# Four-block transformer kernel: residual sums released bank by bank, and the second norm turned per token tile with the router's product between

## Chip, core and metric

The kernel runs on one core of a Trainium2 chip. The metric is the device time of one execution in microseconds (us). The kernel before takes 2551.68 us, the median of three runs from 2546.58 to 2554.73.

## The reference, cut to what matters

The input is 256 tokens of width 1024, all in 32-bit floats. A first block has two layers, each a mixer (gated delta rule, then dilated window attention) and a squared-ReLU MLP. A second block has two layers, each with three gated branches, an output product, and a mixture of 16 experts that choose their tokens. The residual stream `x` goes through a root-mean-square norm ahead of every part:

```
first block:  for i in 0, 1:
    x = x + mixer_i(rmsnorm(x, norm_mix[i]))
    x = x + square(relu(rmsnorm(x, norm_mlp[i]) @ w1)) @ w2
x = rmsnorm(x, norm_final)
second block: for l in 0, 1:
    h  = rmsnorm_2(x, norm1_g[l]) * (1 + sc1) + sh1
    x  = x + g1 * (merged(h) @ w_out[l])
    h2 = rmsnorm_2(x, norm2_g[l]) * (1 + sc2) + sh2
    aff = softmax(h2 @ w_router[l])          # 16 experts
    x  = x + g2 * experts(h2, top_k(aff))    # each expert takes its 32 best tokens
return rmsnorm_2(x, final_g)
```

A norm needs the sum of squares over a token's whole row of 1024 values, so it can't be finished before the last residual sum of that token.

## The kernel before, in words

**Tiles.** The 256 tokens stand as two tiles of 128, token on partition: `X[:, t, :]` is the residual of tile `t`, `XN` its normed copy, `HT` the normed copy turned to features on partitions (eight chunks `dc` of 128 features, 256 tokens wide). PSUM has eight banks of 512 columns. A product that ends in a residual fills banks 0 to 3: bank `b` holds tile `b // 2`, columns half `b % 2`. Its last weight unit is walked bank by bank (L819 to L827, L869 to L891, L1011 to L1028), so that bank 0 is complete first and bank 3 last.

**Weights.** They stream through a ring of six slots of 2 MB, loaded by SyncE's queue (L395 to L401). A slot is loaded anew when its user has raised `w_free`; each expert of the second block takes six units of 2 MB.

**Order of the work.** Each engine has its own instruction stream, written out by hand, and waits on semaphores with counts. VectorE (DVE), ScalarE (ACT), GpSimd (POOL) and TensorE (PE) share a norm as follows. ACT handles tile 0: when `x_half` says that the tile's residual is complete, it squares and sums it (L2016), forms the mean (L2018, `var0`), POOL takes it to the power -1/2 (L2415), and ACT scales the tile (L2033 or L2023, `xn0`). DVE handles tile 1 in the same way: L1332 squares and sums with one instruction over 1024 columns, L1335 forms the mean (`var1`), POOL takes the power, DVE scales (L1342 or L1363, `xn1`). PE turns eight chunks of each tile (`norm`, L565 to L574).

**Residual sums of the first block** (`residual`, L1366 to L1376, four times): DVE waits for `half_mm`, which PE raises when bank 1 is complete, and adds banks 0 and 1 to tile 0. Ahead of bank 2 it waits until the whole weight unit is used (`complete`, that is bank 3), and only then adds banks 2 and 3. After the first and the third residual the norm goes straight to an MLP (`norm_split`, L576 and L1361): tile 0 is turned and multiplied first, tile 1 only behind two products of tile 0. After the second and the fourth, the next step (`norm` for the window attention, the final norm of the first block) wants both tiles.

**Residual sums of the second block** (`gated_residual`, L1782 to L1797): each bank is multiplied by a gate row into `TMP` and then added, two instructions of 512 columns per bank, with a `drain` (`settle`) after each. It runs after the output product (L1926) and after the experts (L2000).

**The second norm** (L1929 to L1932 on DVE, L2374 on ACT, L1244 to L1250 on PE) stands between the output product and the router. DVE first forms the scale and shift columns `SCL` and `BIA`. PE's `norm` turns both tiles into banks 4 to 7, with both tiles of a chunk side by side. ACT applies scale and shift to chunks 0 to 3 and DVE to chunks 4 to 7, 256 columns each (L2037, L1349). PE waits for all eight and then multiplies the router weights: 16 products (tile by chunk) with 16 columns each (L1248), recorded as 32. ACT meanwhile rounds `XN` to a second copy (L2375) and DVE subtracts it (L1935). DVE's L1937 takes the row maximum of the router's result, and from there softmax, top-k, gather and the expert loop (L1273, first product L1284) follow.

## Time and profile before

| | |
|---|---|
| median of three runs | 2551.68 us |
| the profiled execution, its own time | 2548.41 us |
| span of its trace | 2546.4 us |
| PE busy | 2051.8 us, 81% |
| DVE busy | 864.3 us, 34% |
| ACT busy | 594.8 us, 23% |
| POOL busy | 32.0 us, 1% |
| read from memory | 639.21 MB, 251 GB/s over the span |

The span is the time from the first to the last instruction; the 2.0 us to the execution's own time lie around it. Busy shares are averages over stages with different limits. PE's granted clock in the profile is 1.0 at 2.4 GHz and 0.5 at 1.2 GHz.

### The profile page before, as it was taken

Reading aid. Unit: us, or ns where it says so; the run is one execution under the profiler, and the core shown is the slowest. Engines: PE = TensorE matmul, PEld = TensorE weight load, DVE = VectorE, ACT = ScalarE, POOL = GpSimd, SP = SyncE. Lnnn points to the kernel's source line nnn. Section 1 sums busy time; section 2 is a strip of 40 time slices with the busy share of each in tenths; the row PEclk is TensorE's granted clock in tenths of the full one; section 3 lists DMA queues with packets and bytes.
Section 4 is the critical chain, followed back from the end, with each engine's and each line's share of the span. In section 5 each row is a group of like instructions: output and inputs, shape, how many; then the busy total and the mean of one; then the engine's idle time right before and its main releaser. Section 6 shows DMA issues by size and latency. Waiting matters only on the chain.

```text
span 2546.4 us, 34316 instructions
## 1 busy us (share of the span) xinstructions
PE 2051.8 (81%) x14184; PEld 1362.8 (54%) x14184; DVE 864.3 (34%) x1599; ACT 594.8 (23%) x1001; POOL 32.0 (1%) x50
## 2 busy tenths in 40 slices
PE   7877889998998997999876666665999976666765
PEld 6756657877756885788542222222778652222221
DVE  4645564665554664244220000002144230010002
ACT  3222234441123442064210010001054120000000
POOL 0010000000000000000000000000000000000000
PEclk9989899998998998999888887887999988888787
DMA  8201034766963665432459999999332439999996
GB/s 309 102 1 35 2 109 155 265 242 208 329 240 137 251 250 176 149 133 100 165 223 427 426 427 425 426 427 387 134 132 93 201 153 426 427 426 427 426 426 283
DMA packets 150299, 641.76 MB, mean 252 GB/s; under 512 B 9310, under 2 KB 30840, under 8 KB 117046
## 3 DMA queue, kind: packets, MB, share of 16 engines
q1 hardware_dynamic: 143898, 637.13, 63.0%
q10 hardware_dynamic: 6300, 3.20, 0.5%
q8 instruction: 74, 1.21, 0.2%
q14 instruction: 27, 0.22, 0.0%
HBM read 639.21 MB, written 1.10 MB: 251 GB/s over the span
## 4 chain that ended last, share of the span: by engine, by line
PE 55%; DMA 31%; DVE 6%; ACT 3%; issue 2%; DVEq 1%; POOL 1%; SPq 0%; ACTq 0%; POOLq 0%
DMA ring<-in_w_down 31%; PE psum L1189 5%; PE psum L844 5%; PE psum L846 5%; PE psum L845 5%; PE psum L1304 4%; PE psum L1100 3%; PE psum L1089 3%; PE psum L942 3%; PE psum L616 2%; PE psum L1179 2%; PE psum L823 2%; PE psum L647 1%; PE psum L959 1%; PE psum L737 1%
## 5 line engine op out<-in xcount | busy, mean ns | idle before, releaser
L1284 PE MATMUL psum<-ring,arena 128*32 128x256 f32 x4096 | 298.0, 442 | 185.1 <-DMA ring<-in_w_up 146.1
L1284 PEld LDWEIGHTS psum<-ring,arena 128*32 128x32 f32 x4096 | 143.5, 123 | 341.5 <-issue 155.6
L1304 PE MATMUL psum<-ring,arena 128*32 128x512 f32 x1024 | 166.9, 784 | 94.1 <-DMA ring<-in_w_down 84.8
L844 PE MATMUL psum<-arena_r 128*128 128x512 f32 x512 | 207.8, 406 | 13.9 <-DVE arena_r L1650 7.1
L846 PE MATMUL psum<-ring_r,arena_r 128*128 128x512 f32 x512 | 205.0, 400 | 0.0
L1991 DVE TENSOR_TENSOR arena<-psum,arena 128x256 f32<-128x256 f32 x32 | 13.6, 425 | 559.0 <-PE psum L1284 559.0
L1384 DVE TENSOR_TENSOR ring_r<-ring,arena_r 128x2048 fp32r<-128x2048 f32 x64 | 143.8, 2288 | 87.0 <-ACT arena_r L2049 87.0
L2392 ACT ACT_TABLE_LOAD x32 | 41.1, 1283 | 514.3 <-PE psum L1284 514.3
L1998 DVE COPY arena<-psum 128x512 f32<-128x512 f32 x64 | 44.3, 692 | 273.0 <-PE psum L1304 271.8
L2049 ACT CAST arena_r<-ring 128x2048 fp32r<-128x2048 f32 x64 | 119.6, 1904 | 71.8 <-PE psum L846 71.8
L1304 PEld LDWEIGHTS psum<-ring,arena 128*32 128x32 f32 x1024 | 32.8, 126 | 191.4 <-DMA ring<-in_w_down 101.5
L1400 DVE SCALAR_TENSOR_TENSOR arena<-ring,c_act,arena 128x512 f32<-128x512 f32 x168 | 126.3, 752 | 12.5
L1313 PE MATMUL psum<-arena 128*128 128x512 f32 x256 | 127.0, 640 | 0.3
L844 PEld LDWEIGHTS psum<-arena_r 128*128 128x128 f32 x512 | 98.6, 193 | 37.5 <-issue 7.8
L1189 PE MATMUL psum<-x_normed_r,arena_r 128*128 128x256 f32 x384 | 116.5, 303 | 0.2
L846 PEld LDWEIGHTS psum<-ring_r,arena_r 128*128 128x128 f32 x512 | 98.0, 191 | 23.5
L1189 PE MATMUL psum<-x_normed_r,ring_r 128*128 128x256 f32 x384 | 108.5, 282 | 0.0
L1189 PE MATMUL psum<-h_featmajor_r,arena_r 128*128 128x256 f32 x384 | 107.2, 279 | 0.0
L845 PE MATMUL psum<-arena_r 128*128 128x512 f32 x256 | 103.1, 403 | 0.0
L845 PE MATMUL psum<-arena_r,h_featmajor_r 128*128 128x512 f32 x256 | 101.8, 397 | 0.0
L1313 PEld LDWEIGHTS psum<-arena 128*128 128x128 f32 x256 | 49.8, 207 | 92.9 <-issue 50.7
L616 PE MATMUL psum<-h_featmajor,ring 128*128 128x256 f32 x384 | 88.4, 385 | 1.8 <-DVE h_featmajor L1347 1.8
(379 smaller groups left out, 3026.1 us busy)
## 6 DMA issues: line engine op xcount, KB each, us to landing
ring<-in_w_gate SPq DMA_DIRECT2D x64, 2048.0 KB, 26.6
ring<-in_w_up SPq DMA_DIRECT2D x64, 2048.0 KB, 26.1
ring<-in_w_down SPq DMA_DIRECT2D x64, 2048.0 KB, 26.3
ring<-in_mlp_w SPq DMA_DIRECT2D x32, 2048.0 KB, 8.7
ring<-in_w_mod SPq DMA_DIRECT2D x24, 2048.0 KB, 11.2
ring<-in_w_in SPq DMA_DIRECT2D x20, 2048.0 KB, 8.1
ring<-in_gdn_w_in SPq DMA_DIRECT2D x8, 2048.0 KB, 17.9
ring<-in_dswa_w_in SPq DMA_DIRECT2D x9, 1536.0 KB, 14.4
```

The source lines that it names most:

```text
L616: ins = mm(bank(ch % 4, T), W(n, 512)[:, k, (ch % 4) * P:(ch % 4 + 1) * P], HT[:, k, :], start=k == 0, stop=k == KC - 1)
L844: mm(o, xh, wh, start=start, stop=False, skip_group_check=True)
L845: mm(o, xl, wh, start=False, stop=False, skip_group_check=True)
L846: return mm(o, xh, wl, start=False, stop=stop, skip_group_check=True)
L942: ins = mm(bank(n % 4, T), W(u, SCOLS)[:, k, (n % 3) * P:(n % 3 + 1) * P], HT[:, k, :], start=k == 0, stop=k == KC - 1)
L1189: ins = mm(o[:, 0], w[:, k, :], x[:, k, :], start=k == 0 and x is XH_R and w is wh, stop=k == KC - 1 and w is wl, skip_group_check=True)
L1284: ins = mm(PS[32 * j:32 * j + 32, 4 + m, 0:T], XGE[:, 4 * u + kk, :], W(v + 2 * m + u, D)[:, kk, j * T:(j + 1) * T], start=u == 0 and kk = ...
L1304: ins = mm(PS[32 * j:32 * j + 32, (7, 4)[half], :], HTE[:, k % 2, 32 * (k // 2):32 * (k // 2) + 32], W(v + 4 + u, D)[:, j, half * 512:(hal ...
L1313: ins = mm(bank(2 * t + u), S4[:, t * P:(t + 1) * P], YS[:, u, :], start=False, stop=False, skip_group_check=True)
L1384: v.tensor_tensor(ring_r[slot][:, at], ring[slot][:, at], WH[h % 4].bitcast(F32), ALU.subtract).then_inc(sem("w_lo"), 1)
L1400: ins = v.scalar_tensor_tensor(acc, w, CACT[:, k:k + 1], acc, ALU.mult, ALU.add)
L2049: a.copy(WH[h % 4], ring[mlp_unit(l, i) % RING][:, hf * HALF:(hf + 1) * HALF]).then_inc(sem("hi"), 1)
```

## The change

`half_mm` is raised twice per residual, for bank 1 and for bank 2, and DVE waits for each. Bank 2 is now added when it is complete; only bank 3 waits for the whole unit. For tile 1 the square and sum over 1024 columns is split into two of 512 columns (`square_part`), each run behind the sum of its bank; a small addition (`ssq_parts`) joins them in `mean_square`. This is used by the four residuals of the first block and by the output product's residual of the second block; the residual after the experts, the first norm of each layer of the second block, the very first and the very last norm keep the whole square (`parts=False`). In the second block `SCL` and `BIA` of the second norm are formed ahead of the residual. The second norm is turned per token tile (`norm_split` with `pm=True`): tile 0 into banks 4 and 5, tile 1 into banks 6 and 7. ACT scales all eight chunks of tile 0 and chunks 0 to 3 of tile 1, DVE chunks 4 to 7 of tile 1, 128 columns each. PE turns tile 0, then tile 1, then multiplies the router with tile 0, waits for tile 1's chunks, and multiplies the router with tile 1.

```diff
@@ PE: rows_product, mlp down, out_steps alike
-                    if last and (kk, b) == (cnt - 1, 1):
+                    if last and kk == cnt - 1 and b in (1, 2):
                         ins.then_inc(sem("half_mm"), 1)
@@ PE: second norm and router
+                def router(t):
+                    for k in range(KC):
+                        ins = mm(PS[:, 4, t * NE:(t + 1) * NE], HT[:, k, t * P:(t + 1) * P], WR[:, k, :], start=k == 0, stop=k == KC - 1)
+                    return ins
...
-                norm(L * 2 + 5, True)
-                normed(L * 2 + 7)
-                for t in range(TT):
-                    for k in range(KC):
-                        ins = mm(PS[:, 4, t * NE:(t + 1) * NE], HT[:, k, t * P:(t + 1) * P], WR[:, k, :], start=k == 0, stop=k == KC - 1)
-                ins.then_inc(sem("router_mm"), 1)
+                for t in range(TT):
+                    norm_split(L * 2 + 5, t, True)
+                    if t == 1:
+                        pe.wait_ge(sem("ht0_ready"), L + 1)
+                        router(0)
+                pe.wait_ge(sem("ht_ready"), L * 16 + 48 + 16)
+                router(1).then_inc(sem("router_mm"), 1)
@@ DVE: norm
+            def square_part(h):
+                xs = X[:, 1, h * 512:(h + 1) * 512]
+                v.tensor_tensor_reduce(out=XN[:, 1, h * 512:(h + 1) * 512], in0=xs, in1=xs, scale=1.0, scalar=0.0,
+                                       op0=ALU.mult, op1=ALU.add, accum_out=ssq_parts[:, h:h + 1])
+            def mean_square(r, meanwhile=None, parts=True):
+                if parts:
+                    settle()
+                    v.tensor_tensor(ssq[:, 1:2], ssq_parts[:, 0:1], ssq_parts[:, 1:2], ALU.add)
+                else:
+                    v.tensor_tensor_reduce(out=XN[:, 1, :], in0=X[:, 1, :], in1=X[:, 1, :], scale=1.0, scalar=0.0,
+                                           op0=ALU.mult, op1=ALU.add, accum_out=ssq[:, 1:2])
                 settle()
                 v.tensor_scalar(var[:, 1:2], ssq[:, 1:2], 1.0 / D, EPS, ALU.mult, ALU.add).then_inc(sem("var1"), 1)
@@ DVE: residual
-                dve.wait_ge(sem("half_mm"), n)
+                dve.wait_ge(sem("half_mm"), 2 * n - 1)
                 for b in range(4):
                     t, h = b // 2, b % 2
                     if b == 2:
-                        ins.then_inc(sem("x_half"), 1)
+                        dve.wait_ge(sem("half_mm"), 2 * n)
+                    elif b == 3:
                         complete()
                     xs = X[:, t, h * 512:(h + 1) * 512]
                     ins = v.tensor_tensor(xs, bank(b), xs, ALU.add)
-                ins.then_inc(sem("x_ready"), 1)
+                    if b == 1:
+                        ins.then_inc(sem("x_half"), 1)
+                    elif b == 3:
+                        ins.then_inc(sem("x_ready"), 1)
+                    if b >= 2:
+                        settle()
+                        square_part(h)
@@ DVE: gated_residual
                     ins = v.tensor_tensor(xs, xs, TMP, ALU.add)
                     if b == 1:
                         ins.then_inc(sem("x_half"), 1)
+                    elif b == 3:
+                        ins.then_inc(sem("x_ready"), 1)
+                    settle()
+                    if b >= 2 and parts:
+                        square_part(h)
+                    if b == 1:
+                        tile1_first()
+                    elif b == 2:
                         tile1_ready()
-                    elif b < 3:
-                        settle()
-                ins.then_inc(sem("x_ready"), 1)
                 settle()
@@ DVE: second norm
-                dve.wait_ge(sem("half_mm"), L + 5)
-                gated_residual(L * 2 + 1, lambda: (settle(), spent(dve, u2 + V_OUT + 1, tu)))
                 v.scalar_tensor_tensor(SCL, mc(4), 1.0, PMC[:, bass.ds(L * 8 + PM_AT["norm2_g_2"], 8)], ALU.add, ALU.mult)
                 v.tensor_copy(BIA, mc(3))
-                settle()
-                norm(L * 2 + 6, L * 2 + 7, lambda dc: SCL[:, dc:dc + 1], lambda dc: BIA[:, dc:dc + 1])
+                dve.wait_ge(sem("half_mm"), L * 2 + 9)
+                gated_residual(L * 2 + 1, lambda: dve.wait_ge(sem("half_mm"), L * 2 + 10), lambda: spent(dve, u2 + V_OUT + 1, tu), True)
+                mean_square(L * 2 + 6)
+                v.tensor_scalar(XN[:, 1, :], X[:, 1, :], rstd[:, 1:2], None, ALU.mult).then_inc(sem("xn1"), 1)
+                dve.wait_ge(sem("ht_psum"), L * 3 + 9)
+                for dc in range(4, KC):
+                    v.tensor_scalar(HT[:, dc, P:T], PS[:, 7, (dc % 4) * P:(dc % 4 + 1) * P], SCL[:, dc:dc + 1], BIA[:, dc:dc + 1],
+                                    ALU.mult, ALU.add).then_inc(sem("ht_ready"), 1)
@@ ACT: second norm
-                norm(L * 2 + 6, L * 2 + 7, L * 2 + 6, lambda dc: SCL[:, dc:dc + 1], lambda dc: BIA[:, dc:dc + 1])
+                mean_square(L * 2 + 6, L * 2 + 6)
+                act.wait_ge(sem("rstd_ready"), (L * 2 + 6) * 2 + 1)
+                a.activation(XN[:, 0, :], X[:, 0, :], ACT.Copy, scale=rstd[:, 0:1]).then_inc(sem("xn0"), 1)
+                for t in range(TT):
+                    act.wait_ge(sem("ht_psum"), L * 3 + 8 + t)
+                    for dc in range(KC - 4 * t):
+                        ins = a.activation(HT[:, dc, t * P:(t + 1) * P], PS[:, 4 + 2 * t + dc // 4, (dc % 4) * P:(dc % 4 + 1) * P],
+                                           ACT.Identity, scale=SCL[:, dc:dc + 1], bias=BIA[:, dc:dc + 1])
+                        if t == 1:
+                            ins.then_inc(sem("ht_ready"), 1)
+                    if t == 0:
+                        ins.then_inc(sem("ht0_ready"), 1)
                 a.copy(XNH_R, XN[:]).then_inc(sem("xn_hi"), 1)
```

## Rows read from the trace of the kernel before

**Rows 1.** The page, its chain that ended last: shares of the span.
```profile
PE 55%; DMA 31%; DVE 6%; ACT 3%; issue 2%; DVEq 1%; POOL 1%; SPq 0%; ACTq 0%; POOLq 0%
```

**Rows 2.** The same chain in order of time: start us, us, what.
```profile
1225.57 20.70 PE psum L823 x48
...
1338.24 26.59 DMA ring<-in_w_down
```

**Rows 3.** Timeline, layer 0's second norm: start us, us, engine, line, operation [idle before <-releaser].
```profile
1253.15 0.69 DVE L1788 TENSOR_TENSOR arena<-psum,arena 128x512 f32<-128x512 f32 x1 [3.79 <-PE psum L823]
...
1253.92 0.69 DVE L1790 TENSOR_TENSOR x_resid<-x_resid,arena 128x512 f32<-128x512 f32 x1
...
1256.81 1.23 DVE L1332 CUSTOM_DVE_ANT_0 x_normed<-x_resid 128x1024 f32<-128x1024 f32 x1
...
1258.48 0.15 DVE L1335 TENSOR_SCALAR var<-ssq 128x1 f32<-128x1 f32 x1 [0.43 <-issue]
...
1260.10 1.97 PE L573 MATMUL psum<-base,x_normed 128*128 128x128 f32 x8 [6.10 <-DVE x_normed L1342]
1262.11 1.93 ACT L2037 ACTIVATE h_featmajor<-psum,norm_shift,norm_scale 128x256 f32<-128x256 f32 x4 [9.39 <-PE psum L573]
...
1264.10 7.01 PE L1248 MATMUL psum<-arena,h_featmajor 128*128 128x16 f32 x32 [2.02 <-ACT h_featmajor L2037]
...
1265.86 2.29 DVE L1935 TENSOR_TENSOR x_normed_r<-x_normed,arena_r 128x2048 fp32r<-128x2048 f32 x1 [1.85 <-ACT arena_r L2375]
1271.14 0.19 DVE L1937 TENSOR_REDUCE arena<-psum 128x2 f32<-128x32 f32 x1 [2.99 <-PE psum L1248]
```

**Rows 4.** Timeline, DVE: a square of 512 columns elsewhere, and two small instructions with a drain between.
```profile
672.21 0.69 DVE L1695 CUSTOM_DVE_ANT_0 arena<-psum,arena 128x512 f32<-128x512 f32 x1 [1.39 <-PE psum L980]
...
1272.46 0.17 DVE L1939 RECIPROCAL arena<-arena 128x2 f32<-128x2 f32 x1 [1.12 <-ACT act_junk L2380]
1272.70 0.37 DVE L1942 TENSOR_SCALAR arena<-arena 128x16 f32<-128x16 f32 x2
```

**Rows 5.** Timeline, the second residual (ahead of the window attention).
```profile
585.65 1.29 DVE L1375 TENSOR_TENSOR x_resid<-psum,x_resid 128x512 f32<-128x512 f32 x2 [4.29 <-PE psum L846]
...
588.38 0.15 DVE L1335 TENSOR_SCALAR var<-ssq 128x1 f32<-128x1 f32 x1
...
590.00 1.97 PE L573 MATMUL psum<-base,x_normed 128*128 128x128 f32 x8 [3.52 <-DVE x_normed L1342]
```

**Rows 6.** Timeline, the third residual (ahead of the second MLP).
```profile
770.12 2.48 DVE L1375 TENSOR_TENSOR x_resid<-psum,x_resid 128x512 f32<-128x512 f32 x4
...
772.73 1.23 DVE L1332 CUSTOM_DVE_ANT_0 x_normed<-x_resid 128x1024 f32<-128x1024 f32 x1
773.03 1.84 POOL L2415 TENSOR_TENSOR rstd<-var,neg_half 128x1 f32<-128x1 f32 x2 [183.88 <-ACT var L2018]
...
774.39 1.15 ACT L2023 ACTIVATE x_normed<-x_resid,rstd 128x1024 f32<-128x1024 f32 x1 [1.44 <-POOL rstd L2415]
```

**Rows 7.** Timeline, the first residual (ahead of the first MLP).
```profile
378.16 0.56 POOL L2415 TENSOR_TENSOR rstd<-var,neg_half 128x1 f32<-128x1 f32 x1 [21.77 <-ACT var L2018]
...
381.08 2.18 ACT L2027 ACTIVATE arena_r<-psum,param_cols 128x128 fp32r<-128x128 f32 x8 [1.18 <-PE psum L583]
...
382.25 2.16 DVE L1358 SCALAR_TENSOR_TENSOR h_featmajor_r<-psum,param_cols,arena_r 128x128 fp32r<-128x128 f32 x8 [0.57 <-ACT arena_r L2027]
```

**Rows 8.** Stretches of layer 0's second norm: busy us by engine, granted clock, DMA share, GB/s.
```profile
1256.00:1260.00 4.00, 0.00 (x0) 0.00 (x0) 2.55 (x7) 0.00 (x0) 0.55 (x1) 0.73 1.00 422
```

**Rows 9.** Timeline: first expert product of layer 0, row maximum and first expert product of layer 1.
```profile
1299.95 7.11 PE L1284 MATMUL psum<-ring,arena 128*32 128x256 f32 x128 [1.88 <-DVE arena L1984]
...
2048.93 0.19 DVE L1937 TENSOR_REDUCE arena<-psum 128x2 f32<-128x32 f32 x1 [2.99 <-PE psum L1248]
...
2074.93 5.39 PE L1284 MATMUL psum<-ring,arena 128*32 128x256 f32 x96 [1.87 <-DVE arena L1984]
```

**Rows 10.** Timeline, DVE at the start of layer 1, behind the loop's branch.
```profile
1768.07 1.23 DVE L1332 CUSTOM_DVE_ANT_0 x_normed<-x_resid 128x1024 f32<-128x1024 f32 x1 [5.97 <-issue]
```

More of the change, by code:

```diff
@@ L885, in down @@
                         ins = three(bank(b), MTH_R[:, k, ts], MT_R[:, k, ts], wh[:, c], wl[:, c], first and k == 0, last and k == 3)
-                        if last and (b, k) == (1, 3):
+                        if last and k == 3 and b in (1, 2):
                             ins.then_inc(sem("half_mm"), 1)
@@ L1024, in out_steps @@
                              start=i == 0 and kk == 0, stop=i == 2 and kk == 2, skip_group_check=True)
-                    if i == 2 and (b, kk) == (1, 2):
+                    if i == 2 and kk == 2 and b in (1, 2):
                         ins.then_inc(sem("half_mm"), 1)
@@ L1081, in _ @@
                 norm(L * 2 + 4, True)
[L1082 removed]
+                pe.wait_ge(sem("ht_ready"), L * 16 + 48 + 8)
                 def tok(n, w, b):
@@ L1338, in mean_square, with norm @@
                 dve.wait_ge(sem("rstd_ready"), r * 2 + 2)
-            def norm(r, j, scale, shift=None, meanwhile=None):
-                mean_square(r, meanwhile)
+            def norm(r, j, scale, shift=None, meanwhile=None, parts=True):
+                mean_square(r, meanwhile, parts)
                 v.tensor_scalar(XN[:, 1, :], X[:, 1, :], rstd[:, 1:2], None, ALU.mult).then_inc(sem("xn1"), 1)
@@ L1414, in _ @@
             dve.wait_ge(sem("cols_ready"), 4)
-            norm(0, 0, lambda dc: colof("norm_mix", dc))
+            norm(0, 0, lambda dc: colof("norm_mix", dc), parts=False)
             dve.wait_ge(sem("filled"), 1)
@@ L1817, in columns @@
                     v.memset(CZ[:, :, 257:258], 0.0).then_inc(sem("gcol"), 1)
-                norm(L * 2 + 5, L * 2 + 6, lambda dc: SCL[:, dc:dc + 1], lambda dc: BIA[:, dc:dc + 1], meanwhile=columns)
+                norm(L * 2 + 5, L * 3 + 6, lambda dc: SCL[:, dc:dc + 1], lambda dc: BIA[:, dc:dc + 1], meanwhile=columns, parts=False)
                 for t in range(TT):
@@ L1999, in _ @@
                 dve.wait_ge(sem("expert_done"), L * NE + NE + 1)
-                gated_residual(L * 2 + 2, settle)
-            mean_square(9)
+                gated_residual(L * 2 + 2, settle, settle, False)
+            mean_square(9, parts=False)
             dve.wait_ge(sem("fgr_in"), 32)
@@ L2285, in _ @@
                 u2 = U_SEC
-                norm(L * 2 + 5, L * 2 + 6, L * 2 + 5, lambda dc: SCL[:, dc:dc + 1], lambda dc: BIA[:, dc:dc + 1])
+                norm(L * 2 + 5, L * 3 + 6, L * 2 + 5, lambda dc: SCL[:, dc:dc + 1], lambda dc: BIA[:, dc:dc + 1])
                 for dc in range(0, KC, 4):
```

12 lines of the change are left out of this document (4 added, 8 removed).

## The prediction

> **What bounds the kernel now.** I read the page first. The chain that ended last is PE for 55% of the span, DMA for 31%, DVE for 6% [rows 1]: two regimes. In the order of time the DMA part is the expert loop, where each expert waits some 27 us for its last weights [rows 2]; ahead of it everything follows PE, with short pieces of DVE, ACT and POOL wherever a norm stands between two products. So a norm costs what PE idles there, and in the expert loop only the start matters: the ring holds six units, which is one expert, so no further load can begin before the first expert product frees a slot. A start that is earlier by so much shifts the whole DMA-paced loop by as much.
>
> Then the timeline of each norm. In layer 0's second norm the last residual work begins at 1253.15, as PE ends its product, and the row maximum behind the router starts at 1271.14 [rows 3]: 18.0 us, of which PE's turn of tile 1 and the router take 1.97 and 7.01, and the rest is mostly waiting. Layer 1 repeats it: its row maximum stands at 2048.93, at the same distance [rows 9].
>
> **The second norm, part by part (twice).** Before, from 1253.15 to the mean at 1258.48 it is 5.33 us: two multiplications and two additions of 512 columns, at 0.77 each from start to start (1253.15 to 1253.92), `SCL` and `BIA`, and a whole square of 1.23 [rows 3]. After the change, bank 2's pair and its half square run while PE fills bank 3. That cover is real: the last 48 products of L823 take 20.70 us, 0.43 each [rows 2], a bank is 8 of them, 3.4 us, and the three instructions need 3 x 0.77 = 2.3. Were it gone, those 2.3 us would come back. `SCL` and `BIA` go in front of the residual, where DVE waits for PE. What stays behind PE's end: multiplication 0.77, addition 0.77, half square 0.77, small addition 0.24. The half square is priced by the 0.69 of the same instruction over 512 columns plus the drain of 0.08, the small addition by two small instructions with a drain between, 1272.46 to 1272.70 [rows 4]. Together 2.55, so 2.78 is gained. Of the old 5.33, some 0.35 are an idle of 0.43 ahead of the mean that no releaser explains [rows 3] and that may stay: bounds 2.4 and 2.8, taken 2.6.
>
> Then PE. Before, it turns tile 1 (1.97), idles 2.02 until eight chunks are scaled, and runs the router for 7.01 [rows 3]. After, router(0) follows the turn at once, 3.5 us, half of 7.01. Under it ACT and DVE scale four chunks each of 128 columns, 4 x 0.27 = 1.1 by eight of them in 2.18 [rows 7]; so router(1) follows without a gap and the 2.0 us are gone. Tile 0's eight chunks, 2.2 us on ACT, fit between tile 0's turn and tile 1's, where ACT waited 9.39 [rows 3]. The wait for `xn1` now stands at the head of PE's queue with router(0) behind it; that delays the router by nothing against before. ACT's rounding and DVE's subtraction, queued ahead of the row maximum, end later than their old distance: 1.1, 1.8 for the copy (1262.11 + 1.93 to 1265.86) and 2.29 [rows 3], 5.2 behind the turn; the router needs 7.0. They stay covered by 1.8, and are late next. Sum per layer 2.6 + 2.0 = 4.6, for two layers **9.2**. No DMA is issued earlier or later against its own slot, and SP's and POOL's orders stay.
>
> **The four residuals of the first block.** In the second, DVE's two last additions start at 585.65 and the mean at 588.38: 2.73 us, and PE idles 3.52 for it [rows 5]. After: one addition 0.77, half square 0.77, small addition 0.24, together 1.78. Two drains that now stand twice in a row cost about 0.05 each, estimated from the 0.08 between instructions; gain **0.9**. The fourth residual repeats the pattern, ahead of the final norm: another **0.9**. At the first, nothing: DVE waits 0.57 for ACT's tile 0 before it can go on [rows 7], so tile 0's path sets PE's start and tile 1's earlier mean is idle; its price is 0, or up to 0.8 lost if a half square got into POOL's way.
>
> The third is different: DVE comes late, all four additions run in a row from 770.12, and the whole square from 772.73 to 773.96 lies over POOL's power for tile 0, which begins at 773.03. The two powers take 1.84 together where one alone takes 0.56 [rows 6, 7]; ACT goes on at 774.39, 1.36 behind POOL's start. After the change, additions of banks 0 to 2 (0.60 apart) end at 772.0, the half square at 772.8, the fourth addition at 773.5, the second half square starts at 773.6. POOL's 773.03 to 773.59 falls under the addition, which reads PSUM. ACT then starts 0.6 behind 773.03: gain **0.76**. If the second half square catches POOL after all, ACT starts 0.43 behind that square's end, as it does now (773.96 to 774.39), at about 774.75: a loss of 0.36. I take the gain, since the addition is longer than POOL's 0.56; the margin is only 0.04.
>
> Here a rule speaks against the change. The Trainium skill, "GPSIMD Engine Reference", section Key points, says that GpSimd shares its SBUF interfaces with VectorE and contends with VectorE instructions that have two SBUF inputs; the half squares are such. By that rule the trace agrees at the third residual (1.84 against twice 0.56), and if it caught POOL there again the sum would be 1.1 smaller. In the second norm, too, bank 2's addition and half square could hold tile 0's power by up to 2 x 0.77 = 1.5; tile 0 has 9.39 us to spare [rows 3], so it costs nothing there.
>
> **Small losses.** The experts' residual gets a few more drains, 0.1 us at each of two places: -0.2.
>
> **Sum.** 9.2 + 0.9 + 0.9 + 0.76 - 0.2 = 11.6 us. The profiled execution took 2548.41 (span 2546.4), 3.3 below the median of 2551.68; against its own time 2536.8, against the median **2540.1 us**. About 0.3%, 7.7 us, is what a measurement of this kernel can tell from no change, since three runs lie 8 us apart.
>
> **Rivals.**
> *PE's clock stays up (0.15).* In 1256 to 1260 the mean granted clock is 0.73 with PE idle [rows 8]: since the turn of tile 0: it fell from 2.4 to 1.2 GHz at about 1257.8. With a gain of 2.6, tile 1's turn begins at about 1257.5. If the clock holds, turn and router halve (1.0 + 3.5 for 1.97 + 7.01), but the subtraction then bounds: its end moves by 1.0 only, so 1.8 + 1.0 = 2.8 a layer, 5.6 in all: 2534.5. Against it: after an idle of 3.52 the turn took 1.97, the slow value, in the second residual, too [rows 5].
>
> *Part of it is given back (0.20).* From row maximum to first expert product layer 0 takes 28.8 us and layer 1 26.0, with the same instructions [rows 3, 9]. If the changed order puts both layers on the slower side, 2.8 are lost; with POOL caught (1.1) and the idle ahead of the mean kept (0.35 twice) the gain is 7.0: 2544.7. That the change doesn't do what it says, PE leaving the 2.0 us in place in both layers, would give 2544.1 and lies here too.
>
> *Slower, by instruction supply (0.05).* At the start of layer 1, behind the loop's branch, DVE waits 5.97 us for nothing that the profile shows [rows 10], and in the second norm 0.43 in the same way, where the DMA share is 1.00 [rows 3, 8]. DVE's code changes length. If a wait like that of rows 10 came to stand in the second norm in both layers, 11.9 us would be lost, which just outweighs the gain; from the second such wait on the kernel is slower, and with a third at the start of layer 1 it is 17.9 - 11.6 = 6.3 slower: 2558.0. Against it: nothing in the straight code waits longer than 0.43 in the rows. The Trainium skill, "Runtime: NRT & Kernel Launch", section Instruction fetch mechanics, says that crossing a block of instructions in straight code is mostly hidden and that a taken branch to a page not at hand stalls. By that rule the sum stays 2540.1, as both kernels have the same branch; rows 10 agree.
>
> **How the numbers follow.** The forecast has 0.60, the rivals 0.15, 0.20 and 0.05. The scatter of the runs, about 4 to either side, goes on each case. From the clock's 2534.5, less a little, to the partial case's 2544.7 plus 4: range 2532 to 2549. Faster by more than 0.3% is below 2544.0: most of the forecast (0.51 of 0.60), the clock's 0.15 and a quarter of the partial case, 0.70. Within 0.3%: the rest of these, 0.26. Slower by more: 0.04, the last rival with scatter.
>
> **What would show it.** Right: in the second norm the mean 2.6 us behind PE's product instead of 5.3, no idle between the turn of tile 1 and the router, row maximum some 13.4 us behind PE's product end instead of 18.0; PE's idle in the second residual 2.6 instead of 3.52; POOL's first power in the third 0.56 long. Wrong: a wait of several us ahead of DVE's mean, the subtraction ending behind the router, or an expert loop whose first load doesn't start earlier by the same 4.6 us.

## The result, and the profile after

The changed kernel takes **2533.44 us**, the median of six runs from 2523.41 to 2540.30; six runs of the kernel before beside them have 2551.42 (2546.58 to 2554.73). The ratio is 0.9927, with a 95% interval from 0.9905 to 0.9949: some 18 us less. The forecast was 2540.1 in a range of 2532 to 2549. Sign and places were right; the gain is half as large again as the 11.6 us of the sum, and the median lies 1.4 us above the lower end of the range. The profiled execution took 2529.94 us (span 2527.8), 18.5 below the 2548.41 of the execution that was profiled before.

First the second norm of layer 0 in the timeline of the kernel after, which answers to [rows 3], with two lines of layer 1 behind it. PE's product ends as DVE's last multiplication begins, at 1246.02. The columns, here and in the other timelines: start, duration, engine, line, operation, out<-in, count, idle before it and what ended that.

```profile
1246.02 0.69 DVE L1812 TENSOR_TENSOR arena<-psum,arena 128x512 f32<-128x512 f32 x1 [1.16 <-PE psum L823]
1246.79 0.69 DVE L1814 TENSOR_TENSOR x_resid<-x_resid,arena 128x512 f32<-128x512 f32 x1
1247.61 0.69 DVE L1340 CUSTOM_DVE_ANT_0 x_normed<-x_resid 128x512 f32<-128x512 f32 x1
...
1248.43 0.16 DVE L1347 TENSOR_TENSOR ssq<-ssq_parts 128x1 f32<-128x1 f32 x1
1248.67 0.15 DVE L1352 TENSOR_SCALAR var<-ssq 128x1 f32<-128x1 f32 x1
...
1250.30 1.97 PE L583 MATMUL psum<-base,x_normed 128*128 128x128 f32 x8 [3.43 <-DVE x_normed L1960]
1252.06 6.84 PE L1240 MATMUL psum<-arena,h_featmajor 128*128 128x16 f32 x32
...
1252.30 1.37 DVE L1963 TENSOR_SCALAR h_featmajor<-psum,norm_scale,norm_shift 128x128 f32<-128x128 f32 x4 [2.06 <-PE psum L583]
1253.69 1.91 ACT L2418 CAST arena_r<-x_normed 128x2048 fp32r<-128x2048 f32 x1
...
1255.62 2.29 DVE L1967 TENSOR_TENSOR x_normed_r<-x_normed,arena_r 128x2048 fp32r<-128x2048 f32 x1 [1.96 <-ACT arena_r L2418]
1258.94 0.19 DVE L1969 TENSOR_REDUCE arena<-psum 128x2 f32<-128x32 f32 x1 [1.02 <-PE psum L1240]
...
2020.41 1.52 PE L583 MATMUL psum<-base,x_normed 128*128 128x128 f32 x8 [3.43 <-DVE x_normed L1960]
...
2028.61 0.19 DVE L1969 TENSOR_REDUCE arena<-psum 128x2 f32<-128x32 f32 x1 [1.02 <-PE psum L1240]
```

The mean stands 2.65 us behind PE's product end (1246.02 to 1248.67) instead of 5.33. The router begins inside the modelled end of tile 1's turn, with no idle of PE between them. The row maximum comes 12.92 behind the product's end instead of 17.99, and its wait of 1.02 ends with PE: DVE's subtraction, queued ahead of it, is done 1.0 earlier and stays covered as the prediction said, though by 1.0 and not by 1.8. In layer 1 the same distance is 2016.14 to 2028.61, 12.47. There tile 1's turn took 1.52, with a granted clock of 1.00 at its start and 0.50 at its end; in layer 0 it took 1.97 at 0.50 throughout. So the two norms gave 5.07 + 5.52 = 10.6 us.

Then the residuals of the first block, again from the timeline after: the second, which answers to [rows 5], and the third, which answers to [rows 6].

```profile
580.56 0.69 DVE L1393 TENSOR_TENSOR x_resid<-psum,x_resid 128x512 f32<-128x512 f32 x1 [1.29 <-PE psum L846]
581.38 0.69 DVE L1340 CUSTOM_DVE_ANT_0 x_normed<-x_resid 128x512 f32<-128x512 f32 x1
...
582.44 0.15 DVE L1352 TENSOR_SCALAR var<-ssq 128x1 f32<-128x1 f32 x1
...
584.07 1.97 PE L573 MATMUL psum<-base,x_normed 128*128 128x128 f32 x8 [2.67 <-DVE x_normed L1359]
...
765.28 1.88 DVE L1393 TENSOR_TENSOR x_resid<-psum,x_resid 128x512 f32<-128x512 f32 x3
...
767.90 0.69 DVE L1393 TENSOR_TENSOR x_resid<-psum,x_resid 128x512 f32<-128x512 f32 x1
768.20 0.55 POOL L2458 TENSOR_TENSOR rstd<-var,neg_half 128x1 f32<-128x1 f32 x1 [184.97 <-ACT var L2050]
768.72 0.69 DVE L1340 CUSTOM_DVE_ANT_0 x_normed<-x_resid 128x512 f32<-128x512 f32 x1
768.78 1.15 ACT L2055 ACTIVATE x_normed<-x_resid,rstd 128x1024 f32<-128x1024 f32 x1 [0.66 <-POOL rstd L2458]
```

In the second, from the first addition behind PE's product end to the mean it is 1.88 instead of 2.73 (one addition is left there instead of two), and PE idles 2.67 instead of 3.52: 0.85. The fourth repeats it (978.81 to 980.69). In the third POOL's power for tile 0 lies under an addition and takes 0.55 alone; ACT starts 3.50 behind the first addition instead of 4.27: 0.77.

These places sum to 10.6 + 0.85 + 0.85 + 0.77, less 0.1 at each end of the expert loops (the four pairs take 4.72 instead of 4.62 from first to last addition): **12.9 us**. The other 5.6 of the profiled 18.5 lie where the change touches nothing, 4.8 of them ahead of DVE's first addition of the first residual, called the front below: this stretch in the kernel before, in the kernel after, and in the kernel after a second time (its experiment follows), each from its own view of stretches (start:end, length, then busy time of PE, PEld, DVE, ACT and POOL, the granted clock, the DMA share, GB/s).

```profile
9.85:375.25 365.40, 299.80 (x3393) 234.66 (x3394) 202.01 (x491) 99.96 (x275) 17.85 (x21) 0.91 0.26 91
```

```profile
9.77:370.38 360.61, 292.80 (x3393) 228.84 (x3394) 201.90 (x492) 100.03 (x275) 17.85 (x21) 0.92 0.26 93
```

```profile
9.78:376.45 366.67, 298.24 (x3393) 233.41 (x3394) 201.97 (x492) 99.83 (x275) 17.85 (x21) 0.91 0.26 91
```

PE's 3393 products are the same; their busy time and the granted clock are not. The front of the profiled execution had the half clock for less of its time, some 54 us against 68 in the first row and 65 in the third (worked out from the granted clock in slices of 3 us). What that is worth was the main question for the runs.

### The profile page after: what moved, and what is told of

The parts are those of the page before. It is cut to its first block, busy times and chain, and to the rows that moved or that the text cites. A ratio compares the mean times of both kernels' runs of the same rounds, so it can differ in the third digit from the quotient of the medians.

```text
span 2527.8 us, 34370 instructions
## 1 busy us (share of the span) xinstructions
PE 2038.3 (81%) x14184; PEld 1355.8 (54%) x14184; DVE 864.9 (34%) x1617; ACT 599.8 (24%) x1017; POOL 31.3 (1%) x50
## 3 DMA queue, kind: packets, MB, share of 16 engines
q8 instruction: 74, 1.21, 0.2%
## 4 chain that ended last, share of the span: by engine, by line
PE 55%; DMA 32%; DVE 6%; ACT 3%; issue 2%; DVEq 1%; POOL 0%; SPq 0%; ACTq 0%; POOLq 0%
DMA ring<-in_w_down 31%; PE psum L1189 5%; PE psum L844 5%; PE psum L845 5%; PE psum L846 5%; PE psum L1311 4%; PE psum L1100 3%; PE psum L1089 3%; PE psum L942 3%; PE psum L616 2%; PE psum L1179 2%; PE psum L823 2%; PE psum L959 1%; PE psum L647 1%; PE psum L1275 1%
## 5 line engine op out<-in xcount | busy, mean ns | idle before, releaser
L616 PE MATMUL psum<-h_featmajor,ring 128*128 128x256 f32 x384 | 86.6, 379 | 1.8 <-DVE h_featmajor L1364 1.8
## 6 DMA issues: line engine op xcount, KB each, us to landing
ring<-in_w_up SPq DMA_DIRECT2D x64, 2048.0 KB, 26.2
```

The costliest lines, as they stand in the source:

```text
L616: ins = mm(bank(ch % 4, T), W(n, 512)[:, k, (ch % 4) * P:(ch % 4 + 1) * P], HT[:, k, :], start=k == 0, stop=k == KC - 1)
```

## Experiments

The edits are condensed, `...` marks lines that are left out, and each stands against the changed kernel where nothing else is said.

**The changed kernel and the kernel before, each once more.** No edit. Expected of the first:

> The changed kernel once more, for a second trace of it. In the first trace the stretch ahead of the first residual, which the change does not touch, was 4.9 us shorter than before (DVE's first addition at 370.38 instead of 375.25). Theory A (the front scatters from execution to execution with PE's clock, and the change is worth the 12 to 13 us that its own places show): the addition lies anywhere between 369 and 377, and the time about 12 to 18 us under the kernel before. Theory B (the front follows the code: the changed kernel always has it shorter): the addition lies within 0.5 of 370.4 again, and the time 18 us under the kernel before. The places of the change read the same in both: mean 2.65 behind PE's product end and row maximum 12.9 in layer 0, idle of PE ahead of tile 1's turn 2.67 in the second residual.

and of the second:

> The kernel before, for a second trace of it. Theory A: DVE's first addition of the first residual lies anywhere between 369 and 377, and what differs from the first trace of this kernel by more than 0.3 us in any stretch has a different granted clock there. Theory B: it lies within 0.5 of 375.25 again. Ratio 1.000, from 0.997 to 1.003.

The changed kernel took 2534.70 (ratio 0.9942, 0.9921 to 0.9962), the kernel before 2552.42 (1.0005, 0.9993 to 1.0017). The first addition came at 376.45 in the changed kernel, at 376.96 in the kernel before: Theory A. Within the front the same line shows what changed; the two rows are of the two executions of the changed kernel.

```profile
165.76 2.10 PE L737 MATMUL psum<-arena 128*128 128x128 f32 x16 [2.13 <-DVE arena L1619]
```

```profile
166.52 3.41 PE L737 MATMUL psum<-arena 128*128 128x128 f32 x16 [2.13 <-DVE arena L1619]
```

Sixteen equal products take 2.10 at a granted clock of 1.00 or 3.41 at 0.56. The two fronts of the kernel before, 365.4 and 367.1, have the same mean clock of 0.91 to the digits shown, so the difference in the mean that Theory A expected of them did not appear; single lines do differ (the 48 products of L616 take 12.37 and 10.63). Over the fourteen traces of this study the front takes 360.6 to 368.7 us; the kernel before lies inside with 365.4 and 367.1. So the 4.8 us that the front seemed to give were luck of one profiled execution. The places of the change repeat in the mean (2.65) and in PE's idle in the second residual (2.68), but layer 0's row maximum comes 12.18 behind the product's end and not 12.9: tile 1's turn took 1.22 there, at a granted clock near 1, behind the same idle of 3.43.

**The second norm alone.** The first block's residuals are as before:

```diff
 def residual(n, complete):
     dve.wait_ge(sem("half_mm"), 2 * n - 1)
     for b in range(4):
-        if b == 2: dve.wait_ge(sem("half_mm"), 2 * n)
-        elif b == 3: complete()
+        if b == 2: ins.then_inc(sem("x_half"), 1); complete()
...
-        if b >= 2: settle(); square_part(h)
```

> Only the second norm of the two layers is changed (banks released one by one, halved squares, tile 1 turned with the router's first half behind it); the four residuals of the first block are as before. Theory A: the gain is 5.07 + 5.52 = 10.6 us as the two row maxima showed, so 2541 against 2551.5, and the front has the length of one of the other traces by chance. Theory B: the shorter front needs the changed first block, so the front's addition stays at 375.2, and 10.6 us are all. A third theory, that the layers' code alone sets the phase of the front, would give 370.4 there and some 2536.

2539.93 against 2550.70 (ratio 0.9948, 0.9928 to 0.9967): 10.8 by the medians. From bank 0's addition to the row maximum it is 18.54 and 18.46 instead of 24.00, 11.0 us in all, as Theory A has it. The front was a short one (first addition at 371.46), so it needs no changed first block; but the stretch from there to layer 0's second norm was 877.5, 5.6 longer than in the kernel before, and took it back.

**The first block's residuals alone**, measured twice. The second norm goes back to the old order (the edit in part):

```diff
-    for t in range(TT):
-        norm_split(L * 2 + 5, t, True)
-        if t == 1: pe.wait_ge(sem("ht0_ready"), L + 1); router(0)
-    pe.wait_ge(sem("ht_ready"), L * 16 + 48 + 16)
-    router(1).then_inc(sem("router_mm"), 1)
+    norm(L * 2 + 5, True)
+    normed(L * 2 + 7)
+    router(0); router(1).then_inc(sem("router_mm"), 1)
```

> Only the four residuals of the first block are changed (banks released one by one, halved squares); the second norm stays whole, behind the old order of waits, but for its residual's wait, which now counts the bank releases. Theory A: the gain is 0.85 + 0.85 in the second and fourth residual, 0.25 net behind the third (0.77 at its first turn, of which the clock took back 0.5) and 0.24 at the first, 2.2 in all, so 2549; within 0.3 per cent of the kernel before. Theory B: the front is shorter by 4.9 too, 7 us in all, 2544.5. PE's idle in the second residual is 2.67 by both, row maximum 18.0 behind the product's end by both.

> The kernel with only the first block's four residuals changed, once more: its median lay 5.7 us under the kernel before, while its own places show 0.85 + 0.85 + 0.8 there and 0.35 at each second norm (the 0.43 us of idle ahead of the mean was gone), 3.2 in all. Theory A (the rest is scatter of PE's clock in stretches that the code does not touch): the ratio lies between 0.9975 and 0.9995 this time, and the sum over the places is 3.2 again. Theory C (the shorter idles of the first block make the clock come back earlier in what follows, so that the gain is larger than at the places): the ratio is 0.997 to 0.998 again and the time at the half clock between the first residual and layer 0 is smaller than the 60.3 us of the kernel before by 6 or more.

2545.01 against 2550.70 (0.9972, 0.9958 to 0.9985), then 2544.23 against 2551.30 (0.9962, 0.9947 to 0.9976): 5.7 and 7.1 us. The places gave what was expected, 0.85, 0.85 and 0.8, and each row maximum came 23.65 behind bank 0's addition instead of 24.00, as the idle of 0.43 ahead of the mean was gone: 3.2. So the first expectation, 2549, was too slow, and the second, a ratio of at least 0.9975, failed as well. Theory C is not borne out. Time at the half clock between the first residual and layer 0's second norm, worked out from the granted clock in slices of 3 us, is 68 and 58 us here, against 65 in both traces of the kernel before: more in one execution and less in the other. What differs in both is a later stretch, with the same instructions: from layer 0's row maximum to its first expert product it is 28.8 in both traces of the kernel before, and 25.9 and 24.7 here.

**The same stretch reached at another moment.** The kernel before, with products of zeros that move layer 0 and touch nothing behind (the edit against the kernel before, in part):

```diff
+    pe.wait_ge(sem("x_half"), L * 2 + 5)
+    for _ in range(4):
+        mm(bank(0), zero1.to_broadcast([P, P]), zero1.to_broadcast([P, 512]), start=True, stop=False, ...)
     norm(L * 2 + 4, True)
```

> The kernel before, with four products of zeros (512 columns, into bank 0 while it is free) in PE's idle ahead of each layer's first norm, and nothing of the change. The zeros are work added. They move layer 0 earlier by some 1.5 us (the turns of its first norm at the full clock) and leave the code of the second norm and behind it as it was. In both traces of the kernel before, 28.8 us lie between layer 0's row maximum and its first expert product; in the kernels with only the first block changed, 25.9 and 24.7, with the same instructions. Theory A (when the clock comes back in that stretch depends on the moment at which it is reached): the stretch is not 28.8 here, but anything from 24.5 to 29.0; the time 1.5 to 6 us under the kernel before. Rival (it is the kernel before that has 28.8 there, and the change that takes it away): 28.8 within 0.2, and 1.5 us under the kernel before at most. From bank 0's addition to the row maximum 24.00 by both.

2547.28 against 2552.32 (0.9977, 0.9967 to 0.9987). The timeline has the row maximum and the first expert product of both layers:

```profile
1272.03 0.19 DVE L1945 TENSOR_REDUCE arena<-psum 128x2 f32<-128x32 f32 x1 [2.99 <-PE psum L1256]
...
1298.09 7.12 PE L1292 MATMUL psum<-ring,arena 128*32 128x256 f32 x128 [1.88 <-DVE arena L1992]
...
2047.16 0.19 DVE L1945 TENSOR_REDUCE arena<-psum 128x2 f32<-128x32 f32 x1 [2.99 <-PE psum L1256]
...
2076.19 7.12 PE L1292 MATMUL psum<-ring,arena 128*32 128x256 f32 x128 [1.88 <-DVE arena L1992]
```

Layer 0's stretch is 26.06 now, and layer 1's, which was 26.0 before, is 29.03: neither the layer nor the code of the stretch sets its length, and the rival fails. That the moment sets it, as Theory A has it, is not shown: the kernel before reached the stretch at 1271.14 and at 1272.83 and took 28.8 both times, and this one reached it between them. What the clock does there hangs on something earlier that no run isolates. Nor does the stretch explain the time. Both layers together take 55.1 here against 54.8, and the profiled execution, 2549.39, is no shorter than those of the kernel before (2548.41 and 2550.08), so the 5.0 us between the medians have no place in a trace. In the other kernels without moved fills the stretch lies between 24.5 and 29.0.

**The router's two products together again**, behind the wait for all chunks of tile 1:

```diff
     for t in range(TT):
         norm_split(L * 2 + 5, t, True)
-        if t == 1: pe.wait_ge(sem("ht0_ready"), L + 1); router(0)
+    pe.wait_ge(sem("ht0_ready"), L + 1)
     pe.wait_ge(sem("ht_ready"), L * 16 + 48 + 16)
+    router(0)
     router(1).then_inc(sem("router_mm"), 1)
```

> The changed kernel with the router's two products put back together, behind the wait for all chunks of tile 1; everything else stays split per token tile. Theory A (each part of the sum lies on the path): ACT's four chunks behind tile 1's turn take 1.51, with the wait some 1.6 to 2.0 us, and they stand open between turn and router again: PE idle 1.6 to 2.0 there, row maximum 14.5 to 14.9 behind PE's product end instead of 12.9, 3.2 to 4.0 us lost in all, about 2538. Rival (the subtraction or the clock sets the row maximum, not the router's place): row maximum stays within 0.5 of 12.9 and nothing is lost.

2539.53 against 2549.43 (0.9952, 0.9938 to 0.9966). Of the timeline:

```profile
1256.45 1.97 PE L583 MATMUL psum<-base,x_normed 128*128 128x128 f32 x8 [3.43 <-DVE x_normed L1959]
...
1260.11 6.98 PE L1240 MATMUL psum<-arena,h_featmajor 128*128 128x16 f32 x32 [1.69 <-ACT h_featmajor L2411]
1267.12 0.19 DVE L1968 TENSOR_REDUCE arena<-psum 128x2 f32<-128x32 f32 x1 [3.05 <-PE psum L1240]
```

An idle of 1.69 stands ahead of the router, and the row maximum comes 14.94 behind the product's end in layer 0 and 14.47 in layer 1, 2.0 later than in the changed kernel in each. Theory A, at the place. By the medians the total lost more, 6 to 8 us against the three series of the changed kernel instead of 4.0; no place of the change shows the rest.

**Whole squares again**, with the banks still released one by one:

```diff
-    if b >= 2: settle(); square_part(h)
...
 def mean_square(r, meanwhile=None, parts=True):
+    parts = False
```

> The changed kernel with whole squares again, behind the last addition, at the four residuals of the first block and at the second norm; the banks are still released one by one and the router's order stays. Theory A: the mean in layer 0 lies 3.1 behind PE's product end instead of 2.65, PE's idle ahead of tile 1's turn in the second residual is 2.9 instead of 2.67, and POOL's power for tile 0 in the third residual lies under the whole square again, so that it lasts over 1 us and ACT's scaling begins 0.8 later behind the first addition (4.2 instead of 3.5): 0.45 x 2 + 0.25 x 2 + 0.8 = 2.2 lost, which is inside what a measurement can tell. Rival (the halves are worth nothing, bank release is all): mean at 2.65 and POOL at 0.55.

2537.76 against 2549.43 (0.9949, 0.9936 to 0.9961). Layer 0's second norm and the third residual (earlier in time):

```profile
775.90 1.22 DVE L1350 CUSTOM_DVE_ANT_0 x_normed<-x_resid 128x1024 f32<-128x1024 f32 x1
776.21 1.84 POOL L2454 TENSOR_TENSOR rstd<-var,neg_half 128x1 f32<-128x1 f32 x2 [186.99 <-ACT var L2046]
777.57 1.15 ACT L2051 ACTIVATE x_normed<-x_resid,rstd 128x1024 f32<-128x1024 f32 x1 [1.44 <-POOL rstd L2454]
...
1254.77 0.69 DVE L1810 TENSOR_TENSOR arena<-psum,arena 128x512 f32<-128x512 f32 x1 [1.98 <-PE psum L823]
...
1256.41 1.23 DVE L1350 CUSTOM_DVE_ANT_0 x_normed<-x_resid 128x1024 f32<-128x1024 f32 x1 [0.18 <-issue]
...
1258.07 0.15 DVE L1353 TENSOR_SCALAR var<-ssq 128x1 f32<-128x1 f32 x1 [0.43 <-issue]
```

The two powers take 1.84 under the whole square, to the digit what they took in [rows 6], and ACT starts 4.27 behind the first addition again. PE's idle in the second residual is 2.92. All three are Theory A. The mean stands 3.30 behind the product's end, not 3.1: the idle of 0.43 that nothing explains is back. The places lost 3.0 in all (0.7 and 1.1 at the two row maxima, 0.25 twice, 0.8), against 2.2 expected; the median lost 4 to 6 against the series of the changed kernel, which is more than the places show.

**Zeros in PE's idle at the second norm**, to test whether the clock is what makes turn and router slow:

```diff
         norm_split(L * 2 + 5, t, True)
+        if t == 0:
+            for b in (0, 1, 0):
+                mm(bank(b), zero1.to_broadcast([P, P]), zero1.to_broadcast([P, 512]), start=True, stop=False, ...)
```

> The changed kernel with three products of zeros (512 columns each) into a bank that is free and is zeroed again later, between tile 0's turn and tile 1's in both layers, where PE idles 3.43. Nothing else changes; the zeros are work added. Theory A (the clock falls because PE idles there, and the low clock costs the turn 1.0 and the router 3.4): the granted clock stays 1.00 over turn and router, these take 1.0 and 3.4, and the subtraction, whose end moves by 1.0 only, sets the row maximum: 10.9 behind PE's product end instead of 12.9, 2.0 a layer, 4.0 in all. Rival (the products of 16 columns do not hold the clock, it falls within the turn or the router anyway): 11.5 to 12.9 behind, 0 to 1.4 a layer. Rival, slower: at the half clock the three products last 3.9, longer than the idle, and tile 1's turn is late by 0.5.

2529.43 against 2549.43 (0.9924, 0.9911 to 0.9937). Layer 0 in the timeline, and its clock in the view of stretches:

```profile
1252.57 2.75 PE L1255 MATMUL psum<-zero 128*128 128x512 f32 x6
...
1256.17 1.16 PE L583 MATMUL psum<-base,x_normed 128*128 128x128 f32 x8 [0.85 <-DVE x_normed L1964]
1257.16 5.28 PE L1240 MATMUL psum<-arena,h_featmajor 128*128 128x16 f32 x32
...
1260.68 2.29 DVE L1971 TENSOR_TENSOR x_normed_r<-x_normed,arena_r 128x2048 fp32r<-128x2048 f32 x1 [1.96 <-ACT arena_r L2422]
1262.89 0.18 DVE L1973 TENSOR_REDUCE arena<-psum 128x2 f32<-128x32 f32 x1
```

```profile
1256.00:1258.00 2.00, 1.83 (x17) 1.83 (x17) 0.75 (x3) 0.64 (x2) 0.00 (x0) 1.00 0.98 414
1258.00:1260.00 2.00, 2.00 (x16) 2.00 (x15) 0.73 (x3) 2.00 (x4) 0.00 (x0) 0.76 0.37 156
1260.00:1262.00 2.00, 2.00 (x11) 2.00 (x11) 1.31 (x1) 1.94 (x2) 0.00 (x0) 0.50 0.00 0
```

The clock stays up over the turn (1.16 instead of 1.97) and falls inside the router, which takes 5.28. Now the subtraction ends last: the row maximum follows it without a wait, 11.00 behind the product's end in both layers. Theory A in its price (10.9), the first rival in the router's own products. The places give 1.9 and 1.5 us against the first trace of the changed kernel; in time the two kernels can't be told apart (0.9924 here, 0.9926 to 0.9942 there).

**Half of the zero fills moved into that idle**, where they serve a purpose:

```diff
+        if t == 0:
+            for b in (0, 1): mm(bank(b), zero1..., start=True, stop=False, ...)
...
     pe.wait_ge(sem("gr_out"), L * 2 + 2)
-    for b in range(4):
+    for b in (2, 3):
```

> The changed kernel with the zero fills of banks 0 and 1 moved up, from behind the experts' gate into PE's idle between tile 0's turn and tile 1's; the fills of banks 2 and 3 stay. In the changed kernel the eight fill products take 5.18 us, 1267.10 to 1272.28, and the products that spread the picked indices begin as they end, at 1272.21, though DVE had these ready at 1268.91. Theory A: half of the fills, 2.6 us, leaves that path, the spreading products begin at 1269.7 by the old clock, and the two layers gain 2.6 each, 5.2 in all, plus 0 to 1.4 a layer if the fills in the idle hold the clock up in the turn. Rival (the clock takes it back): with fewer products ahead of it the gather of L1275 runs at the half clock for longer, and up to 2.6 a layer is given back: 0.

2533.63 against 2549.43 (0.9922, 0.9907 to 0.9938), no better than the changed kernel although its row maxima come 11.01 and 11.00 behind the product's end. Fills, spreading and gather of layer 0 here, and then the fills of the changed kernel:

```profile
1271.33 3.78 PE L1268 MATMUL psum<-zero 128*128 128x512 f32 x4 [2.08 <-ACT arena L2428]
1275.04 3.78 PE L1271 MATMUL psum<-arena,base 16*128 16x512 f32 x4
...
1279.36 0.63 PE L1278 MATMUL psum<-arena_r,x_normed_r 128*128 128x512 f32 x1
1279.79 0.63 PE L1278 MATMUL psum<-arena_r 128*128 128x512 f32 x1
```

```profile
1267.10 5.18 PE L1265 MATMUL psum<-zero 128*128 128x512 f32 x8 [2.17 <-ACT arena L2425]
```

Four fills take 3.78 here where eight take 5.18 in the changed kernel; the spreading takes 3.78 instead of 1.98, and the gather's products stand 0.43 apart instead of 0.25. The granted clock is 0.50 from 1268 to 1283. From row maximum to first expert product it is 27.8 and 27.9, and that product takes 8.77 instead of 7.11. The rival: the clock took back what the shorter queue gave.

**The changed kernel a third time, and zeros in the idles of four norms.** The second is the experiment with zeros at the second norm, and in addition:

```diff
+def zeros(n):
+    for _ in range(n):
+        mm(bank(0), zero1.to_broadcast([P, P]), zero1.to_broadcast([P, 512]), start=True, stop=False, ...)
...
 def norm(k, pm=False, zero_fills=0):
...
         if t == 1:
+            zeros(zero_fills)
             pe.wait_ge(sem("xn1"), k + 1)
...
+    if l == 1: pe.wait_ge(sem("x_half"), 3); zeros(3)
     norm_split(k_norm, 0)
...
-norm(2)
+norm(2, zero_fills=2)
...
+    pe.wait_ge(sem("x_half"), L * 2 + 5); zeros(4)
     norm(L * 2 + 4, True)
```

> The changed kernel a third time, for a third trace and five more timings. Theory A: the front's addition lies anywhere from 369 to 377, from the first addition of layer 0's second norm to its row maximum 18.2 to 18.9 us, and 18.4 to 18.5 in layer 1, against 24.00 before; the median between 2532 and 2540, as the clock falls.

> The changed kernel with products of zeros (512 columns, into bank 0 while it is free) in PE's idles of four norms: three between the two turns of each second norm as in the run before (4.0 us gained there by the row maxima), two in the second residual, three ahead of the third residual's first turn, four ahead of each layer's first norm. The zeros are work added. Theory A (an idle of PE costs the half clock in the turn and in the products behind it, wherever it stands): the second residual's turn of tile 1 takes 1.0 to 1.2 instead of 1.97, the third's 1.0 instead of 1.94 and its first products of 512 columns run 0.23 apart instead of 0.43, about 2 us; layer 0's first turns take 2.1 instead of 3.45 to 3.68: 4.0 + 0.8 + 0.9 + 2.0 + 1.5 = 9 us under the changed kernel, about 2526. Rival (what the clock keeps here it loses a little later): the turns are shorter, but the stretches from residual to residual are as long as before, and the time is that of the kernel with three zeros at the second norms alone, 2529 to 2530. Rival, slower: fills that last longer than the idle delay the turns.

The changed kernel took 2533.29 (0.9926, 0.9907 to 0.9945), with 18.93 and 18.42 from the first addition of the second norm to the row maximum. Its front was the longest of all, with the first addition at 378.61, outside the 369 to 377 that were expected. The kernel with more zeros took **2523.66** against 2551.30 (0.9883, 0.9863 to 0.9903), some 10 us less than the changed kernel beside it. Its turns in the second and third residual and ahead of layer 0:

```profile
588.59 1.09 PE L579 MATMUL psum<-base,x_normed 128*128 128x128 f32 x8 [0.95 <-DVE x_normed L1374]
...
772.07 1.09 PE L589 MATMUL psum<-base,x_normed 128*128 128x128 f32 x8 [0.45 <-ACT x_normed L2070]
...
986.69 1.95 PE L579 MATMUL psum<-base,x_normed 128*128 128x128 f32 x16
```

1.09, 1.09 and 1.95 instead of 1.97, 1.94 and 3.45 to 3.68 in the changed kernel, and the products behind the third residual stand 0.23 apart from the second on, where they stand 0.43 apart there at first. From the first residual to layer 0's second norm it takes 861.1, against 869.4 to 871.5 in the three traces of the changed kernel. Theory A in sum; in layer 0 the stretch behind the row maximum fell on its long side (28.9) and gave some back. One of the turns proves less than it seems: behind the same idle of 2.67 in the second residual, without zeros, the turn took 1.97 in five traces and 1.09 to 1.21 in three. In the third residual it took 1.94 in every trace without zeros.

## Why the prediction came out as it did

*The second norm, 9.2 us forecast:* this is the term that was mis-sized; it measured 10.6. Its first part, 2.6 for the mean, measured 2.68. The 0.43 of idle ahead of the mean, which the forecast kept in part, was gone altogether. It is not a matter of the whole square: it is there in the kernel before and with whole squares again, but gone with the first block's residuals alone, where the second norm keeps its whole square. Its cause is open. Its second part, 2.0 for PE's idle, measured 2.39 in layer 0 and 2.84 in layer 1: the idle went, as the run with the router put back shows by bringing back 2.0 a layer. In layer 0 the turn was as slow as before, and the rest came from the router, which began 1.76 behind the turn's start, 0.21 before the turn's modelled end, and took 6.84 instead of 7.01. In layer 1 the turn ran partly at the full clock (1.52), and the router began 1.32 behind its start; this part was not forecast, and it depends on the execution, as the same turns took 1.22 to 1.97 in layer 0 and 1.41 to 1.52 in layer 1 in the three traces of the changed kernel. The row maximum, forecast some 13.4 behind the product's end, came 12.92 and 12.47 behind it. Two prices in the forecast were too low and stayed hidden: ACT's eight chunks of tile 0 took 2.90 and not 2.2, its four of tile 1 took 1.51 and not 1.1. With the router ending earlier, that leaves the subtraction 1.0 of cover.

*The residuals, 0.9 + 0.9 + 0.76 and nothing at the first:* measured 0.85, 0.85, 0.77. At the first, 7.50 us lie between the first addition and the first product of the MLP in both kernels. The margin of 0.04 for POOL was none at all, as its power ended at 768.75 and the half square had begun at 768.72; it took 0.55 all the same. That the contention is real where a whole square lies over it was shown by putting it back. The Trainium skill, "GPSIMD Engine Reference", section Key points, has GpSimd contend with VectorE instructions of two SBUF inputs; under the whole square the runs agree (1.84 for the two powers). In the second norm, where up to 1.5 was allowed for bank 2's addition and half square, the power of tile 0 met both and took 0.59, only 0.04 more than alone, in the kernel after:

```profile
1243.36 0.69 DVE L1814 TENSOR_TENSOR x_resid<-x_resid,arena 128x512 f32<-128x512 f32 x1
...
1243.86 0.59 POOL L2458 TENSOR_TENSOR rstd<-var,neg_half 128x1 f32<-128x1 f32 x1 [228.47 <-ACT var L2050]
...
1244.16 0.69 DVE L1340 CUSTOM_DVE_ANT_0 x_normed<-x_resid 128x512 f32<-128x512 f32 x1
```

An addition of two SBUF inputs covers the power's first 0.19 us and a half square its last 0.29. The rows suggest why this cost so little: the power ends 0.40 behind the end of the DVE instruction under which it began, here the addition (1244.05 to 1244.45) as at the third residual the whole square (773.96 to about 774.36, as ACT starts at 774.39 [rows 6]), so what it waits for would be the rest of that one instruction. POOL's spans are rough and no run varied this, so it is argued and not shown.

*The small losses, 0.2:* measured 0.1 at each of two places.

*The sum and the median.* The places make 12.9 against 11.6. The step that failed beyond that is the one that laid the runs' scatter evenly on each case: the three series of the changed kernel are 18.0, 16.0 and 18.0 us under the kernel before beside them, 4 or so more than the places. The runs show where such an excess can come from, PE's clock in untouched stretches, whose length differs from execution to execution (the front) and changes with an edit far ahead of them (28.8 and 26.0 turned into 26.06 and 29.03). Layer 0's stretch behind the row maximum, 28.8 in both traces of the kernel before and 26.2, 24.5 and 26.0 in the three of the changed kernel, accounts for some 3 us in those traces. Whether the change lands better there for a reason of its own, or by luck, is open. The places alone would give 2538.8, close to the forecast of 2540.1; the rest of the way to 2533.44 was not foreseen.

*The rivals.* The clock did not stay up by itself over turn and router: the router takes 6.84 and 6.85, though layer 1's turn had part of it. Held up over the turn by zeros, it did what that rival had worked out, the subtraction bounding, 11.00 behind the product's end where the rival's 2.8 a layer would give 10.6. That part is given back: the rival read the 28.8 and 26.0 as a slow and a fast side of the order; they are neither the layer's nor the order's, and they became 26.2 and 27.6. Waits of several us in DVE's code did not appear; layer 1's start shows 6.03 <-issue, as in [rows 10]. The first expert product of layer 0 moved from 1299.95 to 1285.09, with all that lies ahead of it.

## What to carry to other kernels

Read a change at its places, as the distance between two instructions that bracket it, and judge what the rest of the span does from several traces: here stretches with the same instructions differ by up to 8 us between executions. An idle of PE can cost twice, once as idle and once as the half clock in what follows (a turn of 1.97 instead of 1.16 us behind 3.43 us of idle, though not in every execution); shortening the chain of a norm gains the first, products of zeros in what is left of the idle gain the second. Before work is moved out of a queue, ask whether it kept the clock up for the work behind it.

## What was not expected of the hardware

PE's clock can fall while PE is busy all the time: 0.76 and then 0.50 with 2.00 of 2.00 us busy, in the router's products of 16 columns. And fewer products can take longer: four fills took 3.78 us at a granted clock of 0.50, and eight of the same 3.69 in the second trace of the changed kernel, where the clock was up.
